# The second attention layer's scores as three passes over rounded high and low parts, in a one-core transformer kernel

## What is computed

```python
def latent_attention(hx, hc, w_in, q_norm, w_uq, kv_norm, w_ukv, w_out, cos, sin, need_ctx):
    ...
    def attend(qn, qr, kn, kr, v):
        s = (jnp.einsum("bqhd,bkhd->bhqk", qn, kn)
             + jnp.einsum("bqhd,bkd->bhqk", qr, kr)).astype(F32) * scale
        p = jax.nn.softmax(s, axis=-1).astype(v.dtype)
        return jnp.einsum("bhqk,bkhd->bqhd", p, v)
```

## Time and profile before

| | |
|---|---|
| median of 3 runs | 2527.21 us (2522.06 to 2530.29) |
| the profiled execution | 2527.9 us, its span 2526.6 us |
| TensorE matmuls busy | 2357.1 us, 93% |
| VectorE busy | 1845.5 us, 73% |
| ScalarE busy | 1069.9 us, 42% |
| GpSimd busy | 625.5 us, 25% |
| chain that ended last | TensorE 70%, VectorE 14%, DMA 5%, ScalarE 4% |

### The profile page before, as it was taken

One profiled execution on the slowest core, in us unless ns is written; L12 is line 12 of the kernel. 1 busy time (PEld: TensorE's weight loads), 2 busy tenths in 40 slices (PEclk: granted clock), 3 DMA queues, 4 the chain that ended last, 5 costly groups with the idle time before them and its releaser, 6 DMA issues.

```text
span 2526.6 us, 33463 instructions
## 1 busy us (share of the span) xinstructions
PE 2357.1 (93%) x12399; PEld 1983.8 (79%) x12399; DVE 1845.5 (73%) x3422; ACT 1069.9 (42%) x1910; POOL 625.5 (25%) x408
## 2 busy tenths in 40 slices
PE   7989999999999989999999998999688989899997
PEld 5768999999899989999999986787455767455555
DVE  7899898999999977888888875524666454155554
ACT  3332333333488843333333344321566333344452
POOL 4110367778722232322333302000000100000001
PEclk9999999999999999999999999999899999999999
DMA  6537557788788999999999951121000112000001
GB/s 250 187 133 250 167 185 233 244 249 254 254 311 317 331 360 368 363 338 362 359 370 372 353 191 50 51 67 59 1 1 1 51 46 101 32 19 20 10 1 67
DMA packets 162227, 465.94 MB, mean 184 GB/s; under 512 B 15505, under 2 KB 72977, under 8 KB 159633
## 3 DMA queue, kind: packets, MB, share of 16 engines
q1 hardware_dynamic: 100368, 304.40, 34.3%
q0 software_dynamic: 36864, 134.23, 14.9%
q10 hardware_dynamic: 24832, 25.17, 3.1%
HBM read 411.31 MB, written 52.43 MB: 184 GB/s over the span
## 4 chain that ended last, share of the span: by engine, by line
PE 70%; DVE 14%; DMA 5%; ACT 4%; issue 4%; POOL 2%; DVEq 0%; ACTq 0%
PE psum L427 6%; PE psum L429 5%; PE psum L428 5%; PE psum L571 5%; PE psum L573 5%; PE psum L572 5%; PE psum L435 4%; PE psum L437 4%; PE psum L436 4%; DMA arena<-hidden 4%; PE psum L544 3%; PE psum L863 2%; PE psum L453 2%; POOL weights_low L1955 2%; PE psum L883 2%
## 5 line engine op out<-in xcount | busy, mean ns | idle before, releaser
L940 ACT ACTIVATE weights_high<-arena 128x1024 fp32r<-128x1024 f32 x355 | 374.8, 1056 | 430.1 <-PE psum L573 293.7
L1394 DVE TENSOR_TENSOR weights_low<-arena,weights_high 128x1024 fp32r<-128x1024 f32 x266 | 334.0, 1256 | 217.2 <-ACT weights_high L940 216.3
L435 PE MATMUL psum<-x_high,weights_high 128*128 128x384 f32 x1024 | 351.8, 344 | 27.0 <-POOL weights_low L1955 18.6
L571 PE MATMUL psum<-hidden_high,weights_high 128*128 128x384 f32 x1024 | 344.8, 337 | 11.2 <-DVE hidden_low L1656 8.0
L437 PE MATMUL psum<-x_high,weights_low 128*128 128x384 f32 x1024 | 344.5, 336 | 0.0
L436 PE MATMUL psum<-x_low,weights_high 128*128 128x384 f32 x1024 | 344.2, 336 | 0.0
L573 PE MATMUL psum<-hidden_high,weights_low 128*128 128x384 f32 x1024 | 343.3, 335 | 0.0
L572 PE MATMUL psum<-hidden_low,weights_high 128*128 128x384 f32 x1024 | 343.1, 335 | 0.0
L427 PE MATMUL psum<-x_high,weights_high 128*128 128x512 f32 (+1 forms) x696 | 278.1, 400 | 24.0 <-DVE weights_low L1394 19.0
L1955 POOL TENSOR_TENSOR weights_low<-arena,weights_high 128x1024 fp32r<-128x1024 f32 x89 | 229.0, 2573 | 200.3 <-ACT weights_high L940 199.8
L429 PE MATMUL psum<-x_high,weights_low 128*128 128x512 f32 (+1 forms) x696 | 273.0, 392 | 0.0
(11 more groups left out here) (237 smaller groups left out, 4199.3 us busy)
## 6 DMA issues: line engine op xcount, KB each, us to landing
arena<-in_stream SPq DMA_DIRECT2D x227, 512.0 KB, 4.1
arena<-in_v_rows SPq DMA_DIRECT2D x128, 512.0 KB, 7.1
arena<-in_ada_w SPq DMA_DIRECT2D x48, 512.0 KB, 3.3
hidden<-arena SPq DMA_DIRECT2D x128, 192.0 KB, 4.7
router<-arena SPq DMA_DIRECT2D x12, 2048.0 KB, 10.0
arena<-hidden SPq DMA_DIRECT2D x128, 192.0 KB, 7.8
arena<-router ACTq DMA_DIRECT2D x16, 1536.0 KB, 22.6
arena<-in_pair_w SPq DMA_DIRECT2D x8, 576.0 KB, 3.8
```

Of the source, the lines that this page charges most:

```text
L435: PE.matmul(bank[b][:, 0:N], wh[u % 2][:, k, :], xh[:, k, PICKED:T], start=k == 0, stop=False)
L571: PE.matmul(out, wh[w][:, n, :], hh[:, r, :], start=e == 0, stop=False)
L940: ACT.activation(wh[u % 2], slots[u % RING], AF.Copy).then_inc(*tick("weights_high", u))
L1394: DVE.tensor_tensor(wl[u % 2], slots[u % RING], wh[u % 2].bitcast(F32), ALU.subtract).then_inc(*tick("weights", u))
```

## The change

The scores are made in three passes too. For each 512 or 256 columns, `b_scores` issues high by high, key low by query high, and key high by query low: six instructions for two. To have the parts,

- ScalarE's copies of the keys now go into `kb_high` (fp32r); VectorE then makes `kb_low` from bank 7 and `kb_high` (`k_low`, 2 pieces per step);
- TensorE waits for `k_low`, where it waited for `k_head`, before it writes bank 7 again;
- ScalarE rounds the rotated queries (`q_high`, after `b_exponents` of jobs 3 and 5), VectorE subtracts (`q_low`, before `b_maxima` in jobs 4 and 6);
- the shared 32 rows of the keys are split once, ahead of the loop, in eight small instructions on ScalarE and VectorE which wait for one another, and two VectorE copies (L1842, L1843) go away.

```diff
@@ tensor, project
             elif step == 1:
-                PE.wait_ge(*at("k_head", (pair, 0)))
+                PE.wait_ge(*at("k_low", ("b", pair, 0)))
...
                 else:
-                    PE.wait_ge(*at("k_head", (pair, 1)))
+                    PE.wait_ge(*at("k_low", ("b", pair, 1)))
@@ tensor, b_scores
             if t == 0:
-                PE.wait_ge(*at("roped", ("qh", pair, half)))
-                PE.wait_ge(*at("k_head", (pair, 1)))
-            PE.matmul(SC[j % 2][:, 0:T], qs, ks[:, 0:T], start=True, stop=True)
-            PE.matmul(SC[j % 2][:, T:TC], qs, ks[:, T:TC], start=True, stop=True).then_inc(*tick("scored", ("b", j)))
+                PE.wait_ge(*at("q_low", ("b", pair, half)))
+                PE.wait_ge(*at("k_low", ("b", pair, 1)))
+            for out in (slice(0, T), slice(T, TC)):
+                for n, (qs, ks) in enumerate(((qb_high, kb_high), (qb_high, kb_low), (qb_low, kb_high))):
+                    last = PE.matmul(SC[j % 2][:, out], qs[w][rows, half, t * P:(t + 1) * P], ks[w][rows, half, out],
+                                     start=n == 0, stop=n == 2)
+            last.then_inc(*tick("scored", ("b", j)))
@@ scalar
-            k, q = kh[pair % 2], qh[pair % 2]
+            k, q = kb_high[pair % 2], qh[pair % 2]
...
+        ACT.wait_ge(*at("roped", ("kr", 1)))
+        for i, shared in enumerate((slice(64, 96), slice(0, 64))):
+            ACT.activation(kb_high[1][shared, i, :], kh[0][shared, i, :], AF.Copy).then_inc(*tick("kr_high", i))
+        for i, shared in enumerate((slice(64, 96), slice(0, 64))):
+            ACT.wait_ge(*at("kr_low", i))
+            ACT.activation(kb_high[0][shared, i, :], kb_high[1][shared, i, :].bitcast(F32), AF.Copy).then_inc(
+                *tick("kr_twice", i))
+
+        def q_high(pair, i):
+            ACT.wait_ge(*at("roped", ("qh", pair, i)))
+            ACT.activation(qb_high[pair % 2][head_rows[i], i, :], qh[pair % 2][head_rows[i], i, :], AF.Copy).then_inc(
+                *tick("q_high", ("b", pair, i)))
@@ vector
-        DVE.tensor_copy(kh[1][64:96, 0, :], kh[0][64:96, 0, :])
-        DVE.tensor_copy(kh[1][0:64, 1, :], kh[0][0:64, 1, :]).then_inc(*tick("kr_twice", 1))
...
+        DVE.wait_ge(*at("v_up", 11))
+        for i, shared in enumerate((slice(64, 96), slice(0, 64))):
+            DVE.wait_ge(*at("kr_high", i))
+            DVE.tensor_tensor(kb_low[0][shared, i, :], kh[0][shared, i, :], kb_high[1][shared, i, :].bitcast(F32),
+                              ALU.subtract).then_inc(*tick("kr_low", i))
+        for i, shared in enumerate((slice(64, 96), slice(0, 64))):
+            DVE.wait_ge(*at("kr_low", i))
+            DVE.tensor_copy(kb_low[1][shared, i, :], kb_low[0][shared, i, :].bitcast(F32)).then_inc(*tick("kr_low", 2 + i))
+
+        def k_low(pair, step):
+            w = pair % 2
+            cols, n = (slice(0, T), T) if step == 0 else (slice(T, TC), C)
+            DVE.wait_ge(*at("k_head", (pair, step)))
+            DVE.tensor_tensor(kb_low[w][0:64, 0, cols], bank[7][0:64, 0:n], kb_high[w][0:64, 0, cols].bitcast(F32),
+                              ALU.subtract)
+            DVE.tensor_tensor(kb_low[w][64:P, 1, cols], bank[7][64:P, 0:n], kb_high[w][64:P, 1, cols].bitcast(F32),
+                              ALU.subtract).then_inc(*tick("k_low", ("b", pair, step)))
+
+        def q_low(pair, i):
+            rows, w = head_rows[i], pair % 2
+            DVE.wait_ge(*at("q_high", ("b", pair, i)))
+            DVE.tensor_tensor(qb_low[w][rows, i, :], qh[w][rows, i, :], qb_high[w][rows, i, :].bitcast(F32),
+                              ALU.subtract).then_inc(*tick("q_low", ("b", pair, i)))
...
+            if pair < 7 and j % 8 in (4, 6):
+                q_low(pair + 1, (j % 8 - 4) // 2)
             if j + 2 < B_JOBS:
                 b_maxima(j + 2)
+            if pair < 7 and j % 8 < 2:
+                k_low(pair + 1, j % 8)
```

More of the change, by code:

```diff
@@ L258, in write @@
     b_probt = [[area(first + 3 * half, TC // P, 2 * P) for half in range(2)] for first in (64, 10)]
+    kb_high = [rounded(f"keys{w}_high", first, 2, TC) for w, first in enumerate((32, 35))]
+    kb_low = [rounded(f"keys{w}_low", first, 2, TC) for w, first in enumerate((24, 27))]
+    qb_high = [rounded(f"pair_queries{w}_high", first, 2, T) for w, first in enumerate((62, 8))]
+    qb_low = [rounded(f"pair_queries{w}_low", first, 2, T) for w, first in enumerate((38, 30))]
     rope_rows = (slice(64, 96), slice(32, 64))
@@ L873, in b_scores @@
             pair, half, t = b_job(j)
-            qs = qh[pair % 2][head_rows[half], half, t * P:(t + 1) * P]
-            ks = kh[pair % 2][head_rows[half], half, :]
+            rows, w = head_rows[half], pair % 2
             if j >= 2:
@@ L879, in b_scores @@
                 PE.wait_ge(*at("vp", 11))
+                PE.wait_ge(*at("kr_low", 3))
             if t == 0:
-                PE.wait_ge(*at("roped", ("qh", pair, half)))
-                PE.wait_ge(*at("k_head", (pair, 1)))
-            PE.matmul(SC[j % 2][:, 0:T], qs, ks[:, 0:T], start=True, stop=True)
-            PE.matmul(SC[j % 2][:, T:TC], qs, ks[:, T:TC], start=True, stop=True).then_inc(*tick("scored", ("b", j)))
+                PE.wait_ge(*at("q_low", ("b", pair, half)))
[5 more added lines that the diff above has]
+            last.then_inc(*tick("scored", ("b", j)))
         def b_weigh(pair, two, piece):
@@ L1337, in project @@
                 ACT.wait_ge(*at("k_up", (pair, step)))
-                if pair < 2 and step == 0:
-                    ACT.wait_ge(*at("kr_twice", 1))
                 ACT.activation(k[0:64, 0, cols], bank[7][0:64, 0:n], AF.Copy)
@@ L1360, in scalar @@
             project(0, step)
+            if step in (3, 5):
+                q_high(0, step // 2 - 1)
         b_exponents(0)
@@ L1368, in scalar @@
                 b_exponents(j + 2)
+            if j // 8 < 7 and j % 8 in (3, 5):
+                q_high(j // 8 + 1, j % 8 // 2 - 1)
         ACT.wait_ge(*at("weighed", ("b", 7, 0)))
@@ L1867, in b_gates @@
             DVE.tensor_tensor(gx, bank[6], gx, ALU.mult).then_inc(*tick("b_gated", pair))
-        b_rope(0, 0)
-        b_rope(0, 1)
+        DVE.wait_ge(*at("v_up", 11))
[19 more added lines that the diff above has]
+                              ALU.subtract).then_inc(*tick("q_low", ("b", pair, i)))
+        k_low(0, 0)
+        k_low(0, 1)
+        for i in range(2):
+            b_rope(0, i)
+            q_low(0, i)
         b_maxima(0)
```

## The result

The changed kernel takes 2541.68 us, the median of 8 runs (2535.69 to 2544.12). Beside it, on the same chip, the kernel before took 2525.98 us, also a median of 8. The ratio is 1.0057, with 1.0040 to 1.0073 as its 95% interval: slower by 0.57%, or 10 to 18 us. Forecast were 2533.3 us and 0.24%.

A forecast was written before the change was run, and what follows sets the result against it. TensorE nearly bounds a loop (33.80 of 34.64 us), except a chain of rope, maxima, exponents, normalise. Sum 5.8 + 1.0 + 7 x 0.0 - 0.7 = +6.1 us on 2527.9, less 0.7 to the median: 2533.3 us; range 2528 to 2543.

The forecast's parts named there:

- The clock: TensorE idle 5.3 us before the start's step 1 may halve its clock: from -1.8 to +4.3, taken as +1.0 us.
- The start: First pair's start: step 1 +3.85, step 2 +0.90, second score +1.05; sum +5.8 us.
- The other two terms: In the start: step 2 waits for copy and subtraction, +0.90; `q_high` and `q_low` delay the second score, +1.05.
- A score: Three fp32r passes of 0.23 + 0.117 each take 1.04 us where two whole products took 1.29: -0.25.
- The loop: Each of seven loops: five of eight scores give 1.25 us back, new waits take it; 0.0 us a loop.
- Both new waits: In a loop: step 1 for VectorE's subtractions, +0.95; job 7's transposes for ScalarE's copy behind `q_high`, +0.47.
- The rival of the lost savings: Three scores before the second rotation give nothing, exponents of job 6 being late: +0.75 a loop, 2538.6 us; chance 0.25.
- no shorter scores: Rival: a 256-column pass costs 0.23, so a score takes 1.38, 0.09 more than before: 2546 us; chance 0.07.
- TensorE's list: Rival: new waits are hidden in the loops, 64 scores give 16 us, the start takes 6.8: 2518 us; chance 0.07.
- the shorter pass: Rival: score passes step by 0.21 and 0.11, a score takes 0.97 us: no change, 2530.9 us; chance 0.08.
- The end: Last pair, without projection: a ring of exponents, normalise and maxima decides, 21.92 us for eight jobs instead of 22.66: -0.7.
- the walk's own spread: The summed walk, chance 0.53, from 2529 (no clock fall) to 2538 us; about a quarter lies over 2534.8.

The follow-up runs named there:

- e3: Changed kernel with job 1's weighing ahead of step 1 on TensorE's list in the loops, not behind it: 2536.37 us, ratio to before 1.0022.
- e8: Kernel before the change, with five extra multiplications into bank 6 where TensorE waits in the start: 2525.67 us, ratio to before 0.9988.
- e2: Changed kernel with twelve extra multiplications into unused bank 6 where TensorE waits in the start: 2535.69 us, ratio to before 1.0020.
- e6: Changed kernel, second query rounded behind the copy of job 6's transposes, subtracted behind the maxima, job 7's weighing ahead of the scores: 2535.30 us.
- e1: Changed kernel with one whole product of the rounded high parts in place of the three passes, splits and waits kept: 2545.39 us.
- e7: Changed kernel with the edits of e2 (3 for 5 multiplications after step 0), e3, e5 and e6: 2522.60 us, ratio to before 0.9982.
- e5: Changed kernel with the shared 32 rows split later in the start, first keys copied and subtracted ahead of them: 2534.94 us.

## Why the prediction was right in its mechanism and short in one term

**The clock: the term that failed.** The prediction took +1.0, with +4.3 as the upper bound. With the clock kept at 1.00 in both kernels, the start is 31.50 - 25.84 = 5.66 us longer and the first loop 0.01. Without that it is 10.30 and 1.64. So the clock costs 10.30 - 5.66 + 1.64 - 0.01 = 6.3 us in the profiled execution; in one like e3's, where the third fall ended sooner, it would be 4.7. The prediction looked at one wait, the one ahead of step 1, and priced a fall on step 1 and a part of step 2. That fall came and cost 2.32 us, within its bound of 4.3. It said that the fall which was there before might come or not; it came as well, at 2198.7, for 1.69, as in the kernel before (e8). And there was a third, at 2209, behind the new wait of 2.5 us for VectorE's `q_low` ahead of the second score, which reached 3 us into the first loop and cost 3.92 us in all. That wait was priced as a wait alone, and the bound was built without its fall: this is the step that failed.

**The start, +5.8 forecast, 5.66 measured** (e2 against e8). Step 1 came 3.97 later for the 3.85. The other two terms can't be read one by one in the changed kernel, since the low clock lies on them.

**A score, -0.25 forecast.** From the transposes to the end of the score it was 2.00 (2273.94 to 2275.94) and is 1.76 (2291.09 to 2292.85): -0.24. Inside, it is divided otherwise than I thought: the first pass steps by 0.31 and not 0.23 (2291.72 to 2292.03), the others by 0.23 and 0.12, 1.13 in all, and the transposes ahead of it are 0.08 shorter.

**The loop, 0.0 forecast, +0.06 measured.** By its steps, after the earlier trace rows: step 0 to step 2 +0.79 (forecast +0.70; 4.59 and 3.84), step 2 to the second rotation -0.72 (-0.75), from there to job 7's transposes +0.46 (+0.47; 6.44 for 6.45), to job 8's -0.24 (-0.16), to the next step 0 -0.23 (-0.25). Both new waits were named with their releasers. e3 and e6 take each away alone and get back what the walk says, e1 takes the shorter scores away, and e7 adds up e2, e3, e5 and e6. The rival of the lost savings (+0.75 a loop) falls with the loops' 34.70, that of no shorter scores with e1 and with the 256-column steps of 0.12, that of TensorE's list with the two waits, that of the shorter pass with steps of 0.31 and 0.23 where it had 0.21.

**The end, -0.7 forecast for the last pair.** From the transposes of job 55 to those of job 63 it is 22.09 for 22.66, -0.57. But the walk of the seventh loop had counted its last -0.41 already, which lies in this same stretch; from the last step 0 on, the two give -0.05 together where -0.7 was forecast. So 0.41 was counted twice. The rest of the 0.65 us by which this stretch missed is small sizes: +0.52 for +0.42 up to job 55's transposes, -0.57 for -0.7 behind them.

**Sum.** In the layer, without the clock: 5.66 + 0.01 + 0.31 - 0.05 = 5.9, where 5.1 was forecast; with the clock's 6.3, 12.2. The result lies inside the range, but part of that is luck: it is slower than the walk's own spread, 2529 to 2538, and the range reached to 2543 for the rival of the lost savings, which did not happen. Slower by more than 0.3% had 0.43; "same", with 0.5, was held more likely. What remains between 12.2 and the 15.7 of the medians is not settled beyond this: it is within the interval, and the stretch ahead of the layer alone varied by 9 us among single executions.

## What to carry to other kernels

A shorter matmul is a gain only where TensorE's own list ends last. When operands must be split first, count the bank's way back: copy, then subtraction, must both fit under work that TensorE has in hand, and reordering that work (e3) or the engine's queue (e6) is what turns the saving into time. Walk each wait in a short serial stretch for its effect on the clock, to the end of the stretch and into what follows; where it can't be shortened, useless multiplications into a free bank can pay for themselves, as they did here (e2). All of this together (e7) made the change a gain of 0.18% over the kernel before, and of 0.75% over the changed kernel; against the kernel before with its own clock kept up (e8) the layer is 4.5 us shorter, 278.87 for 283.36. The medians of these two, 2522.60 and 2525.67, agree with it in sign, but their intervals against the kernel before overlap (0.9970 to 0.9994, 0.9975 to 1.0000).

## What the runs showed of the hardware

- Behind 2181.50 to 2184.90 (TensorE busy 0.00 us), 2195.10 to 2198.70 (1.50) and 2205.50 to 2208.90 (0.90) the granted clock went from 2.4 to 1.2 GHz. It stayed there for 6.8, 3.4 and 10.2 us, although TensorE was busy for 2.01 to 3.50 us in each of the rows at half clock. 2.5 us less waiting (e5) left the time at half clock at 20.4 us.
- The same TensorE instructions, at the same times behind step 0 to 0.1 us, had a third fall of 10.2 us in one execution (the changed kernel) and of 6.8 in another (e3), which is 1.6 us of the first loop.
- Twelve added multiplications, 10.3 us in sum, made the start 6.33 us shorter (e2).
- At 2.4 GHz the first of a group of fp32r passes steps by 0.31 us behind transposes, the next with the same 512 columns by 0.23; 256 columns step by 0.12.
- VectorE subtracted from PSUM into fp32r in 0.69 us for 512 columns and 0.42 for 256, so by these two points 0.15 of it does not scale with the columns (256 more columns took 0.27; 0.42 - 0.27).
